# Exchanging rotary halves: from TensorE permutation products to ScalarE copies

## The reference

```
def apply_rope(x, ang):
    x1, x2 = x[..., :half], x[..., half:]
    return concatenate([x1 * cos - x2 * sin, x2 * cos + x1 * sin])
# branch A: heads of 64, halves of 32
qa, ka = apply_rope(qa, ang), apply_rope(ka, ang)
# branch C: RMS norm of each head of 64, with a gain, then axial rope:
# the first 32 dims rotated by row, the last 32 by column, halves of 16
qc = apply_axial_rope(rms_norm(qc, qn), row, col)
kc = apply_axial_rope(rms_norm(kc, kn), row, col)
```

## Time and profile before

| | us |
|---|---|
| median of three runs | 1752.04 |
| the profiled execution | 1752.92 |
| its span | 1751.1 |
| TensorE busy | 1724.7 (98%) |
| VectorE busy | 1173.0 (67%) |
| ScalarE busy | 819.6 (47%) |
| GpSimd busy | 259.8 (15%) |

### The profile page before, as it was taken

The page is one execution under the profiler, slowest core; times in us unless marked ns, Lnnn a source line. Parts: engine busy times, 40 slices in busy tenths (PEclk is TensorE's granted clock), DMA queues, the critical chain, the costliest instruction groups (busy, mean ns, idle before and its releaser), DMA issues.

```text
span 1751.1 us, 36991 instructions
## 1 busy us (share of the span) xinstructions
PE 1724.7 (98%) x14000; PEld 1663.3 (95%) x14000; DVE 1173.0 (67%) x2053; ACT 819.6 (47%) x1316; POOL 259.8 (15%) x255
## 2 busy tenths in 40 slices
PE   9999999999999999999999999999999999999997
PEld 8899999999999998888999999999999788999997
DVE  6667756767665566665886655766566666787754
ACT  5555444444444433545554443444433455654443
POOL 0030000011000203333420001000111433340001
PEclk9999999999999999999999999999999999999999
DMA  7435555555555543332555555555554342555553
GB/s 269 142 112 183 184 180 184 188 183 179 176 172 175 174 162 128 121 124 103 167 181 173 172 176 169 180 170 168 180 174 153 107 157 97 169 181 189 182 183 131
DMA packets 84312, 288.80 MB, mean 165 GB/s; under 512 B 9072, under 2 KB 15984, under 8 KB 83952
## 3 DMA queue, kind: packets, MB, share of 16 engines
q1 hardware_dynamic: 79856, 283.14, 48.9%
q10 hardware_dynamic: 4352, 4.20, 0.8%
HBM read 285.96 MB, written 1.34 MB: 164 GB/s over the span
## 4 chain that ended last, share of the span: by engine, by line
PE 89%; DVE 6%; ACT 4%; issue 1%; DMA 0%; POOL 0%; SPq 0%; ACTq 0%; DVEq 0%
PE PS L861 27%; PE PS L863 27%; PE PS L862 27%; DVE w_lo L1513 2%; PE PS L1370 1%; PE PS L1334 1%; ACT S_all L737 1%; ACT w_hi L453 1%; PE PS L1374 1%; PE PS L1298 0%; PE PS L1342 0%; DMA raw<-stream 0%; PE PS L1055 0%; DVE PT L2099 0%; DVE PT L2098 0%
## 5 line engine op out<-in xcount | busy, mean ns | idle before, releaser
L1513 DVE TENSOR_TENSOR w_lo<-raw,w_hi 128x1024 fp32r<-128x1024 f32 x525 | 656.1, 1250 | 301.1 <-ACT w_hi L453 291.1
L861 PE MATMUL PS<-x_hi,w_hi 128*128 128x272 f32 (+1 forms) x2832 | 819.5, 289 | 2.3 <-DVE w_lo L1513 2.2
L863 PE MATMUL PS<-x_hi,w_lo 128*128 128x272 f32 (+1 forms) x2832 | 810.2, 286 | 0.0
L862 PE MATMUL PS<-x_lo,w_hi 128*128 128x272 f32 (+1 forms) x2832 | 808.2, 285 | 0.0
L453 ACT ACTIVATE w_hi<-raw 128x1024 fp32r<-128x1024 f32 x525 | 551.3, 1056 | 518.3 <-PE PS L863 512.7
L861 PEld LDWEIGHTS PS<-x_hi,w_hi 128*128 128x128 f32 x2832 | 535.4, 189 | 8.9 <-issue 4.2
L863 PEld LDWEIGHTS PS<-x_hi,w_lo 128*128 128x128 f32 x2832 | 535.7, 189 | 0.0
L862 PEld LDWEIGHTS PS<-x_lo,w_hi 128*128 128x128 f32 x2832 | 534.7, 189 | 0.7
L861 PE MATMUL PS<-a_hi,w_hi 128*128 128x272 f32 (+1 forms) x1280 | 364.8, 285 | 1.3 <-DVE a_lo L2136 1.3
L863 PE MATMUL PS<-a_hi,w_lo 128*128 128x272 f32 (+1 forms) x1280 | 363.8, 284 | 0.0
L862 PE MATMUL PS<-a_lo,w_hi 128*128 128x272 f32 (+1 forms) x1280 | 362.9, 284 | 0.0
(11 more groups left out here) (302 smaller groups left out, 1241.2 us busy)
## 6 DMA issues: line engine op xcount, KB each, us to landing
raw<-stream SPq DMA_DIRECT2D x525, 512.0 KB, 3.3
biasB<-rpbz ACTq DMA_DIRECT2D x16, 256.0 KB, 3.2
G<-b1mats SPq DMA_DIRECT2D x2, 1024.0 KB, 6.7
h<-xT SPq DMA_DIRECT2D x4, 272.0 KB, 5.5
out<-qk SPq DMA_DIRECT2D x4, 256.0 KB, 3.1
mat<-mats SPq DMA_DIRECT2D x1, 952.0 KB, 5.4
v_tok<-u_rows SPq DMA_DIRECT2D x4, 142.0 KB, 3.2
mat<-u_rows SPq DMA_DIRECT2D x4, 142.0 KB, 4.0
```

Of the source, the lines that this page charges most:

```text
L861: pe.matmul(ps, hi, rh, start=first, stop=False)
L862: pe.matmul(ps, hi, rl, start=False, stop=False)
L863: return pe.matmul(ps, lo, rh, start=False, stop=last)
L1513: dve.tensor_tensor(w_lo[:, slot, :], raw[:, slot, :], w_hi[:, slot, :].bitcast(F32), ALU.subtract).then_inc(lo_done, 1)
```

## The change

The permutation products, their matrices and their events go. ScalarE copies each raw tile in four pieces of 32 partitions, each to the neighbouring group of 32, into a buffer of its own (`swap_tile`, ten of them in the gates' tile G): one tile a turn (`SWAP_AT`), behind the square of that turn. To make 32-partition pieces enough for the axial halves of 16 as well, the channels of qC and kC are reordered on the host (`AXIAL`), as are gains and tables. For A tiles VectorE multiplies the exchanged tile by the sine (from SBUF, in turns 4 and 18 to 21). For C tiles the copy is taken before normalisation, so VectorE normalises the exchanged tile as well as the plain one, with the root read from PSUM twice and a second column of gains; GpSimd multiplies it by the axial sine, a third operation a tile. GpSimd's order is now kA, qA 0 to 3, kC, qC 0 to 3. The gate output of chunk 10, which overwrites the buffers, waits for all ropes.

```diff
+SWAP_ORDER = [0, 5, 6, 7, 8, 9, 1, 2, 3, 4]
+SWAP_AT = {2: 0, 3: 5, 13: 6, 14: 7, 15: 8, 16: 9, 17: 1, 18: 2, 19: 3, 20: 4}
+ROPE_AT = {4: [0], 18: [1], 19: [2], 20: [3], 21: [4]}
-QKV_EVENTS = {0: [("stat", 0)], 4: [("swapA", R_KA)], 16: [("sumC", 0)]}
+QKV_EVENTS = {0: [("stat", 0)], 16: [("sumC", 0)]}
-    QKV_EVENTS[17 + _t] = [("swapA", R_QA + _t)]
-QKV_EVENTS[22] = [("swapC", r) for r in C_TILES]
+QKV_EVENTS[20] = [("castC", i) for i in range(5)]
...
@@ ScalarE
+    def swap(k):
+        act.wait_ge(out_free, ob + (o + (0, 16, 17, 18, 19, 1, 12, 13, 14, 15)[k] + 1))
+        for g in range(4):
+            act.activation(swap_tile(k)[32 * g:32 * g + 32, :], qk[32 * (g ^ 1):32 * (g ^ 1) + 32, ROPE_TILES[k], :],
+                           ACT.Copy).then_inc(swapped, 1)
...
-    mm = pe.matmul(PS[:, b, 0:L], perm, qk[:, i, :], start=True, stop=True)
...
@@ VectorE
+    def rope(k):
+        swap_there(k)
+        dve.tensor_tensor(swap_tile(k), swap_tile(k), mat[:, M_TAB + L:M_TAB + 2 * L], ALU.mult).then_inc(swap_scaled, 1)
...
-    dve.tensor_tensor(G[:, 17 + swaps % 3, :], PS[:, b, 0:L], mat[:, tab + L:tab + 2 * L], ALU.mult)
...
+    swap_there(5 + i)
+    dve.scalar_tensor_tensor(swap_tile(5 + i), swap_tile(5 + i), col[:, gs], PS[:, b, 0:L],
+                             ALU.mult, ALU.mult).then_inc(swap_scaled, 1)
     dve.scalar_tensor_tensor(qk[:, r, :], qk[:, r, :], col[:, gn], PS[:, b, 0:L],
                              ALU.mult, ALU.mult).then_inc(aux_free, ax.up())
...
@@ GpSimd
+    for k, i in enumerate(ROPE_TILES):
+        tab = M_TAB + (0 if k < 5 else 2 * L)
+        pool.wait_ge(swap_scaled, l * ROPES + SCALED_AT[k] + 1)
+        if k >= 5:
+            pool.wait_ge(aux_free, l * LAYER_A + (B1_AUX + CASTC_IN_LAYER + k - 5 + 1))
+            step(pool.tensor_tensor(swap_tile(k), swap_tile(k), mat[:, tab + L:tab + 2 * L], ALU.mult))
         step(pool.tensor_tensor(qk[:, i, :], qk[:, i, :], mat[:, tab:tab + L], ALU.mult))
+        pool.tensor_tensor(qk[:, i, :], qk[:, i, :], swap_tile(k), ALU.add).then_inc(roped, 1)
```

More of the change, by code:

```diff
@@ L30 @@
 LAM_INIT = 0.2
+AXIAL = np.r_[0:16, 32:48, 16:32, 48:64]
+ACROSS = (np.arange(HD) + HD // 2) % HD
 BLK = 8
@@ L58 @@
 C_TILES = [R_KC] + [R_QC + t for t in range(4)]
-QKV_EVENTS = {0: [("stat", 0)], 4: [("swapA", R_KA)], 16: [("sumC", 0)]}
+ROPE_TILES = [R_KA] + [R_QA + t for t in range(4)] + C_TILES
+ROPES = len(ROPE_TILES)
+SCALED_AT = {0: 0, 1: 1, 2: 2, 3: 3, 5: 4, 6: 5, 7: 6, 8: 7, 9: 8, 4: 9}
+SWAP_ORDER = [0, 5, 6, 7, 8, 9, 1, 2, 3, 4]
+SWAP_AT = {2: 0, 3: 5, 13: 6, 14: 7, 15: 8, 16: 9, 17: 1, 18: 2, 19: 3, 20: 4}
+ROPE_AT = {4: [0], 18: [1], 19: [2], 20: [3], 21: [4]}
+QKV_EVENTS = {0: [("stat", 0)], 16: [("sumC", 0)]}
 for _t in range(6):
     QKV_EVENTS[7 + _t] = [("v", _t)]
-for _t in range(4):
-    QKV_EVENTS[17 + _t] = [("swapA", R_QA + _t)]
-QKV_EVENTS[20] += [("castC", i) for i in range(5)]
-QKV_EVENTS[22] = [("swapC", r) for r in C_TILES]
+QKV_EVENTS[20] = [("castC", i) for i in range(5)]
 QKV_EVENT_LIST = [e for t in range(QKV_T) for e in QKV_EVENTS.get(t, [])]
@@ L104 @@
 C_QN = C_G + 9 * KD
-C_SINK = C_QN + 2 * LAYERS
+C_SINK = C_QN + 4 * LAYERS
 C_CONVB = C_SINK + 9 * LAYERS
@@ L116 @@
 NC = C_RW + KD * 20
-M_ID, M_ONES, M_PA, M_PC = 0, P, 2 * P, 3 * P
-M_SEL16 = 4 * P
+M_ID, M_ONES = 0, P
+M_SEL16 = 2 * P
 M_SEL4 = M_SEL16 + 9 * 17
@@ L234, in router_cols, with swap_tile @@
             return S_f[:, 1664 + at:1664 + at + n]
+        def swap_tile(k):
+            return G[:, 10 + k, :]
         gates_bc = Gf[:, 0:16 * SEQ].rearrange("p (e t) -> p e t", e=16)
@@ L250, in build @@
         c_squared, c_rstd, roped = sem("c_squared"), sem("c_rstd"), sem("roped")
+        swapped, swap_scaled = sem("swapped"), sem("swap_scaled")
         scores_out, logits_ready, exp_done, rden_ready = (
@@ L392, in _ @@
                 sp.dma_start(raw[:, s, :], stream[s]).then_inc(raw_landed[s], 16)
-            sp.dma_start(mat[:, 0:M_PA], mats[:, 0:M_PA]).then_inc(ones_landed, 16)
+            sp.dma_start(mat[:, 0:M_SEL16], mats[:, 0:M_SEL16]).then_inc(ones_landed, 16)
             def reload(n, slot):
@@ L401, in _ @@
                 reload(n, n % RING)
-            sp.dma_start(mat[:, M_PA:M_TAB], mats[:, M_PA:M_TAB]).then_inc(consts_landed, 16)
+            sp.dma_start(mat[:, M_SEL16:M_TAB], mats[:, M_SEL16:M_TAB]).then_inc(consts_landed, 16)
             sp.dma_start(alibi, b1mats[:, 0:2048].rearrange("p (h t k) -> p h t k", h=4, t=2)).then_inc(alibi_landed, 16)
@@ L727, in _ @@
                         act.activation(G[:, e, :], qk[:, R_OF[kind] + i, :], ACT.Square).then_inc(c_squared, 1)
+                    if t in SWAP_AT:
+                        swap(SWAP_AT[t])
                 c, o = c + QKV_T, o + QKV_T
@@ L1267, in _ @@
             assert ax.n == B1_AUX, (ax.n, B1_AUX)
-            castC_at = B1_AUX + CASTC_IN_LAYER
             for l in range(LAYERS):
@@ L1289, in _ @@
                         b = aux_begin()
[L1290 to L1297, removed]
-                            mm = pe.matmul(PS[:, b, 0:L], perm, qk[:, i, :], start=True, stop=True)
-                        elif what == "v":
+                        if what == "v":
                             pe.wait_ge(out_free, ob + (o + 6 + i + 1))
@@ L1978, in _, with swap_there @@
                 c, o = FFN_C, FFN_UP + KD
-                swaps = 0
+                def swap_there(k):
+                    dve.wait_ge(swapped, l * 4 * ROPES + 4 * (SWAP_ORDER.index(k) + 1))
+                def rope(k):
+                    swap_there(k)
+                    dve.tensor_tensor(swap_tile(k), swap_tile(k), mat[:, M_TAB + L:M_TAB + 2 * L], ALU.mult).then_inc(swap_scaled, 1)
                 for t, (kind, i) in enumerate(QKV_ORDER):
@@ L1992, in _ @@
                         dve.tensor_tensor(dst, ps, rstd[:, 0:n], ALU.mult).then_inc(out_free, 1)
+                    for k in ROPE_AT.get(t, []):
+                        rope(k)
                     for what, i in QKV_EVENTS.get(t, []):
@@ L2016, in _ @@
                             r = C_TILES[i]
-                            gn = bass.ds(l * 2 + C_QN + (1 if i == 0 else 0), 1)
+                            gn, gs = (bass.ds(l * 4 + C_QN + x + (1 if i == 0 else 0), 1) for x in (0, 2))
+                            swap_there(5 + i)
+                            dve.scalar_tensor_tensor(swap_tile(5 + i), swap_tile(5 + i), col[:, gs], PS[:, b, 0:L],
+                                                     ALU.mult, ALU.mult).then_inc(swap_scaled, 1)
                             dve.scalar_tensor_tensor(qk[:, r, :], qk[:, r, :], col[:, gn], PS[:, b, 0:L],
@@ L2103, in gate_out @@
                     dve.wait_ge(chunk_used, cb + (c + j + 1))
+                    if j == 10:
+                        dve.wait_ge(roped, l * ROPES + ROPES)
                     dve.tensor_tensor(G[:, j, 0:nt], PS[:, j % 2, 0:nt], rstd[:, 0:nt], ALU.mult).then_inc(out_free, 1)
@@ L2253, in _ @@
                 sum_squares(ob + FFN_UP)
[L2255 to L2259, removed]
+                for k, i in enumerate(ROPE_TILES):
[4 more added lines that the diff above has]
+                        step(pool.tensor_tensor(swap_tile(k), swap_tile(k), mat[:, tab + L:tab + 2 * L], ALU.mult))
                     step(pool.tensor_tensor(qk[:, i, :], qk[:, i, :], mat[:, tab:tab + L], ALU.mult))
-                    pool.tensor_tensor(qk[:, i, :], qk[:, i, :], G[:, 17 + n % 3, :], ALU.add).then_inc(roped, 1)
+                    pool.tensor_tensor(qk[:, i, :], qk[:, i, :], swap_tile(k), ALU.add).then_inc(roped, 1)
                 for s in range(PAIRS):
@@ L2311, in constants @@
     p = np.arange(P)
-    c[(p + 32) % 64 + p // 64 * 64, M_PA + p] = 1.0
-    c[(p + 16) % 32 + p // 32 * 32, M_PC + p] = 1.0
     for t in range(8):
@@ L2331, in constants @@
     (cr, sr), (cc, sc) = table(32, row), table(32, column)
-    for k, a in enumerate((cosA, sinA, np.concatenate([cr, cc]), np.concatenate([sr, sc]))):
+    for k, a in enumerate((cosA, sinA, np.concatenate([cr, cc])[AXIAL], np.concatenate([sr, sc])[AXIAL])):
         c[:, M_TAB + k * L:M_TAB + (k + 1) * L] = np.concatenate([a, a])
@@ L2423 @@
         qa, ka, va, qb, kb, vb, qc, kc, vc, gates = np.split(w, np.cumsum([512, 128, 128, 512, 512, 512, 512, 128, 128]), axis=1)
+        kc, qc = (x.reshape(D, -1, HD)[:, :, AXIAL].reshape(D, -1) for x in (kc, qc))
         for part in (ka, kc, kb, va, vc, vb, qc[:, pairs], qa[:, pairs], qb, gates):
@@ L2446 @@
     for l in range(LAYERS):
-        col[:, C_QN + 2 * l] = np.tile(a["qnorm_c_2"][l], 2)
-        col[:, C_QN + 2 * l + 1] = np.tile(a["knorm_c_2"][l], 2)
+        for k, name in enumerate(("qnorm_c_2", "knorm_c_2")):
+            g = a[name][l][AXIAL]
+            col[:, C_QN + 4 * l + k] = np.tile(g, 2)
+            col[:, C_QN + 4 * l + 2 + k] = np.tile(g[ACROSS], 2)
         col[:, C_SINK + 9 * l:C_SINK + 9 * l + 8] = a["sink_a_2"][l][None, :]
```

## The result

The changed kernel takes 1764.92 us (median of four runs, 1764.4 to 1765.7) against 1752.2 for the kernel before: ratio 1.0075, interval 1.0063 to 1.0086. It is 12.7 us slower, and outside the range I gave (1746.5 to 1757.5); the forecast was 1751.5, no change. The profiled execution has a span of 1762.6 us.

A forecast was written before the change was run, and what follows sets the result against it. Bound by TensorE in the QKV stage, then for one or two attention steps by a ScalarE, VectorE and GpSimd chain. Layers -0.9 and +0.3 take 1752.92 to 1752.3; the median, 0.9 lower, gives 1751.5 us, range 1746.5 to 1757.5.

The forecast's parts named there:

- Removed work: TensorE, QKV stage: 20 exchange products at 0.46 us go, 9.2 us, all on the path.
- Price of a copy: ScalarE: each 32-partition copy 0.32 us with overlap (bounds 0.1 and 0.43), a group of four 1.3 us.
- Rival B: ScalarE's copies don't overlap, 0.43 us each; layers cost +1.3 and +2.5, 1755.8 us in all; chance 0.26.
- The ring: Turns 13 to 15, high split, low split, output, square: 3.0 to 4.3 us; sum of squares waits 0.6 and 1.1.
- Root, reads and fifth spread: VectorE's later root and ten spread reads instead of five: TensorE's fifth spread stalls 1.7 us, layer 1 2.3 to 2.6.
- the second ring: Turns 17 to 20: VectorE waits for ScalarE, whose copy groups wait for VectorE's outputs; no size of its own.
- GpSimd's tail: Start of attention: 15 axial operations behind tile 4, 11.0 + 2.4 us, delay first probabilities; TensorE's first transposes wait for GpSimd.
- Rival C: ScalarE copies at a quarter of the cost, 0.1 us each, no ring or late root: near 1747.5 us; chance 0.07.

The follow-up runs named there:

- The last kernel: Changed kernel with copies ahead of the square, GpSimd's axial tiles between attention steps, qA 1 to 3 copies a turn later, VectorE multiplies moved: 1743.95 us, ratio 0.9957.
- the run with the pieces: Changed kernel with four other sets of copies by tile, varying start partition, columns and crossing, exchange left out: one execution, 1753.38 us, only ScalarE's timeline used.
- straight: Changed kernel with one 128-partition copy a tile in place of four of 32 partitions, exchange left out: 1750.62 us, ratio 0.9997.
- the run with filled waits: Changed kernel with 37 idle TensorE products put into its three waits of each layer, all waits kept: 1756.99 us, ratio 1.0032.

## Why the prediction was wrong

- **Removed work, 9.2 us.** Right. The last kernel, in which the new waits are gone, gets 7.5 of it, and the fall of its clock described at the end costs 1.7.
- **Price of a copy: the step that failed first.** I took 0.32 because eight squares in a row show it, and those all start at partition 0. The copies measured 0.455, beyond my upper bound of 0.43, which I had named as a sign of being wrong: without overlap there is 0.02 to 0.03 between two as well, and the overlap is lost with both neighbours. The group with its neighbours costs 2.27 against 1.63. My Rival B had the mechanism and said that it decides from 0.36 on; I gave it 0.26, less than the forecast. The Trainium skill states a like rule in VectorE: DVE Perf Modes, Two Vector instructions with no wait between them, for VectorE alone; the run with the pieces shows its like on ScalarE (0.28 apart with different starts, 0.15 with the same).
- **The ring.** Right in kind, too small in size: 4.97 a turn instead of 4.3, waits for the squares of 1.9 and 2.4 instead of 0.6 and 1.1. That it, and not the load of ScalarE, is the cost is shown by the run with the copies ahead of the square: 7.7 us for a change of order, and the waits for the squares gone.
- **Root, reads and fifth spread.** 3.1 and 2.2 against 1.7 and 2.5. Only the first is much off; the root is later than forecast, but no run separates that from the rest. The 3.0 us by which attention was to start earlier doesn't follow from its terms either: 4.6 + 0.2 - 0.6 - 1.7 - 0.25 is 2.3. That the second ring through turns 18 to 20 is what makes VectorE late here I had in my schedule (VectorE "waits for ScalarE, whose groups wait for outputs") but counted as given; the last run shows it to be avoidable.
- **GpSimd's tail.** Right: 13.7 us for 15 operations against 13.4, and TensorE waits for it at the first transposes, 3.0 and 4.4. Its worth, with the slow clock behind the waits, is 7.0 us.
- **The clock: the missing step.** I priced each wait by its length and put what comes behind it at nothing, without a reason. Behind five of the six waits TensorE ran at 1.2 GHz for some 3 to 5 us, and this costs 7.5 us (by some 3 uncertain), about half of the loss. The rows of before had a hint that it need not: TensorE idles 2.5 of 10 us at 1380 to 1390 with clock 1.00. The length of a wait doesn't settle it: the clock falls behind waits of 2.2 to 4.4 us, and behind one of 0.42 (`straight`), and not behind one of 1.95. With copies at 0.43 and no clock term Rival B gave a loss of 3.8 us; the run with filled waits, which has the waits and not the slow clock, loses 5.6.
- **The same time by other terms.** With one cheap copy a tile the time is 1750.6 against 1751.5 forecast. This is luck and does not bear the sum out: there a tile costs ScalarE some 0.33 us and not the 1.3 of my forecast, the waits for the squares that I had are not there, and the clock takes 5.7 us that I did not have. By its price of copies `straight` is nearer to Rival C (1747.5).

## What to carry to other kernels

Before pricing small instructions of ScalarE by a run of large ones, compare their start partitions: here copies that begin on different groups of 32 partitions paid their full length, and so did their neighbours. Put added work of a helper engine into its wait, ahead of the instruction that others wait for, not behind it; here that order alone was worth about half of the loss. Where the main engine gets a new wait, price a slow clock behind it as well, and count a queue's new tail (here GpSimd's) from the engine that next needs that queue.

## What I had not expected of the hardware

The filled waits: more products, less time. And in the fastest kernel the clock falls once without any wait: TensorE is busy all of 1350 to 1360 and the clock of the stretch is 0.83; the fall comes at 1350.6, as five spreads end whose products have only 10 rows:

```profile
1340.00:1350.00 10.00, 10.00 (x86) 8.94 (x87) 9.90 (x17) 7.93 (x14) 4.34 (x4) 1.00 0.51 168
1350.00:1360.00 10.00, 10.00 (x72) 9.59 (x72) 7.89 (x15) 3.17 (x5) 4.08 (x5) 0.83 0.38 130
```

It costs 1.7 us (10 x 0.17). Layer 0 of the same kernel has the same five spreads and no such fall, nor has the kernel before at this place. But the kernel before has one elsewhere, of which the prediction made nothing: early in its first block the clock is 0.50 from 30 to 32 us, with TensorE busy throughout, shortly behind sixteen products of two columns.

```profile
27.33 1.84 PE L971 MATMUL PS<-mat,S_all 128*128 128x2 f32 x16
...
30.00:32.00 2.00, 2.00 (x11) 2.00 (x11) 1.69 (x11) 0.69 (x2) 0.00 (x0) 0.50 0.94 299
```

So an idle TensorE is not needed for a fall; why it falls at one such place and not at another stays open. The profiled executions have one or two falls of the clock before 160 us, at places that differ from one to the next, of about 1.7 us each: two single executions that differ by less than 2 us show nothing by that.
